# WKV preparation reordered as a pipeline over four channel blocks, with elementwise products on GpSimd

## The reference, cut to what matters

```python
kk = (k * p['k_k']).reshape(B, T, H, N)
kk = kk / jnp.maximum(jnp.linalg.norm(kk, axis=-1, keepdims=True), 1e-12)
for d in range(2):
    w = jnp.exp(-DECAY_SCALE * jax.nn.sigmoid(p['decay_w0'][d] + jnp.tanh(xw @ p['decay_w1'][d]) @ p['decay_w2'][d]))
    a = jax.nn.sigmoid(p['aaa_a0'][d] + (xa @ p['aaa_a1'][d]) @ p['aaa_a2'][d])
    kd = k * (1.0 + (a - 1.0) * p['k_a'])
    y_sum = y_sum + wkv7_scan(rh, w, kdh, vh, -kk, kk * ah, reverse=(d == 1))
    bonus = bonus + jnp.sum(rh * kdh * p['r_k'], axis=-1, keepdims=True) * vh
```

## Time and profile before

| | before |
|---|---|
| median of 3 runs | 2770.46 us |
| lowest, highest | 2763.62, 2773.02 us |
| the profiled execution | 2771.89 us |
| its span | 2770.1 us |
| its mean granted TensorE clock | 0.892 of full speed |
| TensorE matmuls busy | 2271.1 us (82%) |
| VectorE busy | 1157.1 us (42%) |
| ScalarE busy | 763.7 us (28%) |
| GpSimd busy | 334.7 us (12%) |
| stage `prep` | about 562 to 802 us of the span |

### The profile page before, as it was taken

One profiled execution on the slowest core, in us unless ns is written; L12 is line 12 of the kernel. 1 busy time (PEld: TensorE's weight loads), 2 busy tenths in 40 slices (PEclk: granted clock), 3 DMA queues, 4 the chain that ended last, 5 costly groups with the idle time before them and its releaser, 6 DMA issues. The chain is left out here.

```text
span 2770.1 us, 42284 instructions
## 1 busy us (share of the span) xinstructions
PE 2271.1 (82%) x17252; PEld 1898.2 (69%) x17252; DVE 1157.1 (42%) x1619; ACT 763.7 (28%) x1236; POOL 334.7 (12%) x352
## 2 busy tenths in 40 slices
PE   3899997944414768887579986969999999999999
PEld 2788882322203545555568865869999889999987
DVE  4343006646742356767357743422333223332221
ACT  3111110024413214444334422213222212222211
POOL 0000000000000019950544310000000000000000
PEclk9999999966756679999589956989999999999999
DMA  2222210024367210010377424432222333222222
GB/s 85 75 86 86 86 71 35 0 88 193 151 228 222 80 61 1 1 46 11 99 171 186 115 76 148 141 125 76 76 76 80 109 115 111 71 75 76 76 98 89
DMA packets 140716, 262.87 MB, mean 95 GB/s; under 512 B 11024, under 2 KB 89360, under 8 KB 138992
## 3 DMA queue, kind: packets, MB, share of 16 engines
q1 hardware_dynamic: 140592, 261.12, 28.8%
HBM read 189.18 MB, written 68.93 MB: 93 GB/s over the span
## 5 line engine op out<-in xcount | busy, mean ns | idle before, releaser
L203 PE MATMUL ff_acc<-normed_nh,ff_low 128*128 128x320 f32 x1408 | 436.1, 310 | 18.9 <-DVE ff_low L2318 17.7
L204 PE MATMUL ff_acc<-normed_nl,ff_high 128*128 128x320 f32 x1408 | 435.8, 310 | 0.0
L205 PE MATMUL ff_acc<-normed_nh,ff_high 128*128 128x320 f32 x1408 | 435.7, 309 | 0.0
L2318 DVE TENSOR_TENSOR ff_low<-ff_raw,ff_high 128x1024 fp32r<-128x1024 f32 x132 | 161.7, 1225 | 451.6 <-ACT ff_high L2280 451.4
L203 PEld LDWEIGHTS ff_acc<-normed_nh,ff_low 128*128 128x128 f32 x1408 | 264.9, 188 | 19.7 <-issue 19.7
L204 PEld LDWEIGHTS ff_acc<-normed_nl,ff_high 128*128 128x128 f32 x1408 | 265.0, 188 | 0.0
L205 PEld LDWEIGHTS ff_acc<-normed_nh,ff_high 128*128 128x128 f32 x1408 | 264.9, 188 | 0.0
L2280 ACT CAST ff_high<-ff_raw 128x1024 fp32r<-128x1024 f32 x132 | 138.0, 1046 | 255.4 <-PE ff_acc L205 234.0
L204 PE MATMUL ff_acc<-ff_low,ff_hh 128*128 128x512 f32 x440 | 171.2, 389 | 0.0
L203 PE MATMUL ff_acc<-ff_high,ff_hl 128*128 128x512 f32 x440 | 171.2, 389 | 0.0
L205 PE MATMUL ff_acc<-ff_high,ff_hh 128*128 128x512 f32 x440 | 171.2, 389 | 0.0
(11 more groups left out here) (250 smaller groups left out, 4296.8 us busy)
## 6 DMA issues: line engine op xcount, KB each, us to landing
dram_sx<-pr_sx SPq DMA_DIRECT2D x8, 2816.0 KB, 8.1
ff_raw<-in_w_gate SPq DMA_DIRECT2D x44, 512.0 KB, 3.2
ff_raw<-in_w_up SPq DMA_DIRECT2D x44, 512.0 KB, 3.2
ff_raw<-in_w_down SPq DMA_DIRECT2D x44, 512.0 KB, 3.5
si_ab<-dram_sx SPq DMA_DIRECT2D x44, 384.0 KB, 6.9
pj_packed<-in_w_in SPq DMA_DIRECT2D x24, 512.0 KB, 4.3
ch_ops<-dram_sx SPq DMA_DIRECT2D x88, 128.0 KB, 3.5
ch_ops<-dram_sx SPq DMA_DIRECT2D x44, 256.0 KB, 4.5
```

Of the source, the lines that this page charges most:

```text
L203: nc.tensor.matmul(out, ll, rh, start=start, stop=False)
L204: nc.tensor.matmul(out, lh, rl, start=False, stop=False)
L205: return nc.tensor.matmul(out, lh, rh, start=False, stop=stop)
L2318: nc.vector.tensor_tensor(low[s][:, :], raw[s][:, :], high[s][:, :].bitcast(F32), ALU.subtract).then_inc(cut_low[s], 1)
```

## The change

It rewrites the stage `prep`. In it:

- Priming of the semaphores is dropped; counts start at zero.
- VectorE starts each block with the scans and sums of both directions; the bonus of the block before stands behind them; then come the two products `kd` by `k`, then the packed results. The norm `kk` of the next block (`norm_k`) is issued between the results of direction 1, and `floor` and `invert` of the next block ahead of and within direction 0.
- ScalarE takes over the affine step of `kd` (`scale_a`, an Identity activation), puts the square of the next block between the exponentials of the two directions, and runs `root`, `to_rows`, the four sigmoids and the two affine steps of the next block behind the exponentials. The exponential that `r` is multiplied by goes to `sg[d]`, so that `e1` is gone.
- GpSimd takes `av` times `kk` for both directions, `kd[0]` plus `kd[1]`, and the product of that with `r`: four full-width operations a block. The weight `r_k` is folded into four copies of `heads` (`heads_rk`) once at the start.
- SyncE loads `k` and `r` apart from `v`, the first `k` and `r` ahead of the constants; the load for block f+2 is issued behind the stores of block f; the bonus of f is stored in block f+1; each direction's store has a semaphore of its own.

```diff
@@ sync
-                    for d in range(2):
-                        sp.wait_ge(ready, PRIMED + 2 * f + d + 1)
-                        sp.dma_start(g.sx[d, f], ...).then_inc(stored, 16)
-                    sp.wait_ge(bonus, PRIMED + f + 1)
-                    sp.dma_start(g.bonus[f * P:(f + 1) * P, :], kds[:, :]).then_inc(stored, 16)
+                def load_kr(f):
+                    s = f % 2
+                    if f >= 2:
+                        sp.wait_ge(ready, 2 * (f - 1))
+                        sp.wait_ge(kd_summed, f - 1)
...
+                sp.wait_ge(zeroed, 6)
+                load_kr(0)
...
+                load_v(0)
+                load_kr(1)
+                load_v(1)
                 for f in range(FT):
+                    if f >= 1:
+                        store_bonus(f - 1)
+                        if f + 1 < FT:
+                            load_v(f + 1)
+                    for d in both:
+                        sp.wait_ge(ready, 2 * f + d + 1)
+                        sp.dma_start(g.sx[d, f], sx[d][:, :, :, :].rearrange("p c x t -> p (c x t)")).then_inc(sx_stored[d], 16)
+                    if f + 2 < FT:
+                        load_kr(f + 2)
@@ gpsimd
+                for f in range(FT):
+                    s = f % 2
+                    pool.wait_ge(normed, f + 1)
+                    for d in both:
+                        pool.wait_ge(affine, 2 * f + d + 1)
+                        nc.gpsimd.tensor_tensor(av[d][:, :], kk[:, :], av[d][:, :], ALU.mult).then_inc(av_ready, 1)
+                    pool.wait_ge(kd_ready, f + 1)
+                    if f:
+                        pool.wait_ge(bonus_stored, 16 * f)
+                    nc.gpsimd.tensor_tensor(kds[:, :], kd[0][:, :], kd[1][:, :], ALU.add).then_inc(kd_added, 1)
+                    pool.wait_ge(kd_added, f + 1)
+                    pool.wait_ge(kr_in[s], KR * (f // 2 + 1))
+                    nc.gpsimd.tensor_tensor(kds[:, :], r[s][:, :], kds[:, :], ALU.mult).then_inc(kd_summed, 1)
@@ tensor
+                for_w(0, 0)
+                for_a(0, 0)
+                pe.wait_ge(consts, 80)
+                pe.wait_ge(fixed, 1)
+                square_sums(0)
+                for_w(0, 1)
+                for_a(0, 1)
+                spread_norms(0)
                 for f in range(FT):
                     if f + 1 < FT:
                         square_sums(f + 1)
+                        for_w(f + 1, 0)
                         spread_norms(f + 1)
+                        for_a(f + 1, 0)
+                        for_w(f + 1, 1)
+                        for_a(f + 1, 1)
+                    bonus_of(f)
@@ scalar
+                def exponentials(f, d):
+                    act.wait_ge(summed, 2 * f + d + 1)
+                    nc.scalar.activation(tot[:, d, :], tot[:, d, :], ACT.Exp, scale=-DECAY)
+                    nc.scalar.activation(ex[d][:, :], ex[d][:, :], ACT.Exp, scale=-DECAY).then_inc(exped, 1)
+                    nc.scalar.activation(sg[d][:, :], cs[d][:, :], ACT.Exp, scale=-DECAY).then_inc(exped, 1)
+                    act.wait_ge(exped, 4 * f + 2 * d + 2)
+                    nc.scalar.activation(cs[d][:, :], cs[d][:, :], ACT.Exp, scale=DECAY).then_inc(scaled_up, 1)
...
                 for f in range(FT):
+                    more = f + 1 < FT
+                    exponentials(f, 0)
+                    if more:
+                        square(f + 1)
+                    exponentials(f, 1)
+                    if more:
+                        root(f + 1)
+                        to_rows(f + 1)
+                        sigmoid_w(f + 1, 0)
+                        sigmoid_a(f + 1, 0)
+                        sigmoid_w(f + 1, 1)
+                        sigmoid_a(f + 1, 1)
+                        for d in both:
+                            scale_a(f + 1, d)
@@ vector
+                def norm_k(f):
+                    dve.wait_ge(kr_in[f % 2], KR * (f // 2 + 1))
+                    dve.wait_ge(spreads, f + 1)
...
                 for f in range(FT):
+                    sums_of(f, 0)
+                    if f == 0:
+                        floor(0)
+                    sums_of(f, 1)
+                    if f == 0:
+                        invert(0)
+                        norm_k(0)
+                    else:
+                        bonus_of(f - 1)
+                    for d in both:
+                        dve.wait_ge(affine, 2 * f + d + 1)
+                        last = tt(kd[d][:, :], kd[d][:, :], k[s][:, :], ALU.mult)
+                    last.then_inc(kd_ready, 1)
+                    if more:
+                        floor(f + 1)
+                    for d in both:
...
+                        tt(g.etot[:, d, f, :], tot[:, d, :], keep[:, d, :], ALU.mult)
+                        nc.vector.scalar_tensor_tensor(out=o(d, "a"), in0=chunked(kk), scalar=-1.0, in1=chunked(ex[d]),
+                                                       op0=ALU.mult, op1=ALU.mult).then_inc(a_made, 1)
+                        if d == 0 and more:
+                            invert(f + 1)
+                        dve.wait_ge(av_ready, 2 * f + d + 1)
+                        tt(o(d, "b"), chunked(av[d]), chunked(cs[d]), ALU.mult)
+                        if d == 1 and more:
+                            norm_k(f + 1)
+                        dve.wait_ge(kd_ready, f + 1)
+                        tt(o(d, "k"), chunked(kd[d]), chunked(cs[d]), ALU.mult)
+                        tt(o(d, "r"), chunked(r[s]), chunked(sg[d]), ALU.mult).then_inc(ready, 1)
+                bonus_of(FT - 1)
```

More of the change, by code:

```diff
@@ L539, in prep @@
         psa, psb, psq = c.ps("psa", (P, 3 * 512)), c.ps("psb", (P, 3 * 512)), c.ps("psq")
-        consts, zeroed = c.sem("consts"), c.sem("zeroed")
-        loaded = [c.sem(f"loaded{s}") for s in range(2)]
+        consts, zeroed, fixed = c.sem("consts"), c.sem("zeroed"), c.sem("fixed")
+        kr_in, v_in = ([c.sem(f"{n}{s}") for s in range(2)] for n in ("kr_in", "v_in"))
         squared, sums, floored, rooted, inverted, rows, spreads, normed = (
             c.sem(n) for n in ("squared", "sums", "floored", "rooted", "inverted", "rows", "spreads", "normed"))
[L545 to L549, removed]
+        w_prod, a_prod, sig_w, sig_a, affine = (c.sem(n) for n in ("w_prod", "a_prod", "sig_w", "sig_a", "affine"))
+        scanned, mirrored, summed, exped, scaled_up, ready = (
+            c.sem(n) for n in ("scanned", "mirrored", "summed", "exped", "scaled_up", "ready"))
+        kd_ready, av_ready, kd_added, kd_summed, bonus_prod, bonus = (
+            c.sem(n) for n in ("kd_ready", "av_ready", "kd_added", "kd_summed", "bonus_prod", "bonus"))
+        sx_stored = [c.sem(f"sx_stored{d}") for d in range(2)]
+        bonus_stored, a_made = c.sem("bonus_stored"), c.sem("a_made")
         par = lambda name, off: cut(g.par_sb, PCOLS[name] + off, 1)
         chunked = lambda t: t[:, :].rearrange("p (c t) -> p c t", t=CH)
+        both = (0, 1)
+        KR, V = 80, 32
         c.callback(c.reset)
@@ L597, in product, with for_w, for_a @@
                     last.then_inc(sem, 1)
+                def for_w(f, d):
+                    pe.wait_ge(kr_in[f % 2], KR * (f // 2 + 1))
+                    if d or f == 1:
+                        pe.wait_ge(sig_w, 2 * f + d)
+                    elif f >= 2:
+                        pe.wait_ge(bonus, f - 1)
+                    product(psb, w2[f % 2][:, 2 * d, :], g.hid[:, 2 * d, :], w_prod)
+                def for_a(f, d):
+                    if d:
+                        pe.wait_ge(sig_a, 2 * f + 1)
+                    elif f:
+                        pe.wait_ge(normed, f + 1)
+                    product(psa, w2[f % 2][:, 2 * d + 1, :], g.hid[:, 2 * d + 1, :], a_prod)
@@ L607, in spread_norms, with bonus_of @@
+                    pe.wait_ge(sig_a, 2 * max(f, 1))
+                    if f:
+                        pe.wait_ge(normed, f)
                     spread(nc, psa, q, ident, PTOK).then_inc(spreads, 1)
-                pe.wait_ge(consts, PRIMED + 80)
+                def bonus_of(f):
+                    pe.wait_ge(kd_summed, f + 1)
+                    if f + 1 < FT:
+                        pe.wait_ge(sig_w, 2 * f + 4)
+                    else:
+                        pe.wait_ge(bonus, f)
+                    product(psb, heads_rk[:, f, :], kds, bonus_prod)
@@ L616, in _ @@
[L616 to L621, removed]
                     if f + 1 < FT:
                         square_sums(f + 1)
-                    pe.wait_ge(sig_w, PRIMED + 2 * f + 2)
@@ new lines, in sigmoid_a, with scale_a @@
+                def sigmoid_a(f, d):
+                    act.wait_ge(a_prod, 2 * f + d + 1)
+                    if f:
+                        act.wait_ge(ready, 2 * (f - 1) + d + 1)
+                    nc.scalar.activation(av[d][:, :], psa[:, 0:PTOK], ACT.Sigmoid, bias=par("aaa_a0", d * FT + f)
+                                         ).then_inc(sig_a, 1)
```

(25 more changed lines are left out.)

153 lines of the change are left out of this document (66 added, 87 removed).

## The result

| | before | after |
|---|---|---|
| median of 6 runs | 2770.45 us | 2751.24 us |
| lowest, highest | 2763.62, 2773.02 | 2743.68, 2758.86 |
| the profiled execution, its span | 2771.89, 2770.1 | 2743.68, 2741.9 |
| stage `prep`, first fill of padding to first instruction of `solve_in` | 240.0 us | 218.2 us |
| TensorE's granted clock in the stage | 0.64 | 0.55 |

The ratio is 0.993, with a 95% interval of 0.991 to 0.995: 19 us faster where 42 were forecast, and 3 us beyond the slow end of the range. The six runs lie up to 15 us apart, and the profiled execution is the fastest of them, 7.6 us under their median. So I measure on the stage, where the two profiles differ by 21.9 us; another 6.3 us between the two profiled executions lie outside it, where the kernels are the same.

What follows compares the result with a forecast made beforehand. VectorE, the fullest engine, stood idle in a ring of norms, sigmoids, sums, exponentials and results. New blocks of 41.3 us end the stage at 759.8, not 802.2: 2771.9 - 42.4 = 2729.5, less 1.4 gives 2728.1 us; range 2696 to 2748.

Steps and rivals of the forecast that it cites:

- The products' time: TensorE's gate and decay products: 2.36 us apart, the first gate product 2.5; last gate sigmoid ends at T+5.8.
- the ring: Per-block chain from norm through products, sigmoids, exponentials, square and sums to `floor`: 35.4 us without GpSimd's effect on VectorE.
- VectorE's list: VectorE's own work per block: 38.2 us less 8.0 leaves 30.2; about 41.3 with GpSimd's four operations counted in.
- Blocking: In each block, VectorE stands while nearly every GpSimd operation is served: four times 2.8 us.
- the sum of the prediction, 41.4: VectorE's time per block: 30.2 us of work plus four GpSimd operations at 2.8 each.
- GpSimd's operation: One elementwise operation of 1408 columns on GpSimd: 2.9 us, bounds 2.2 and 3.9, giving 2717 and 2745 us.
- The start: Start of the stage: first `k`, `r` land at 570, first scan at 574.2, block 0 ends at 627.1.
- The tail: End of the stage: next stage starts 9.2 us after the last bonus store is issued, at 759.8.
- SyncE's queue: Load of `k`, `r` behind both stores arrives just in time; if 4 us late, two blocks become 2 longer.
- no blocking: Rival: GpSimd's reads fit between VectorE's, blocks take 35.4 us, stage 73.6 less, 2697 us; chance 0.13.
- A smaller gain: Rival: GpSimd operation near 3.9 us, or late loads and bonus stores costing 4 to 10 us; 2740 to 2755; chance 0.12.
- a reordering that doesn't take hold: VectorE still awaits the next norm 5 us or more, `floor` being late through ScalarE; about 2743; no chance of its own.

Runs made afterwards that it cites:

- short products: Changed kernel with the four decay and gate products covering 704 of 1408 columns from block 1 on; blocks 41.7 and 41.6 us, stage 209.9 us.
- experiments two and five: Changed kernel with GpSimd's four operations on 16 columns: stage 192.2 us; changed kernel with those four operations back on VectorE: stage 204.4 us, one run 2730.7 us.
- the run with the last order and a warm TensorE: Changed kernel plus earlier square, decay product first, four operations on VectorE, six added matmuls behind the spread; blocks 38.0 us, stage 191.5 us.

## Why the prediction was wrong

The direction was right and the size was not: the stage was forecast at 197.6 us and took 218.2, 20.6 more. Step by step:

- **The products' time: the step that failed.** The prediction took 2.36 us from the spacing of two sigmoids and carried it to places where TensorE would be doing other things just before. Those rows were made at a clock of 0.94 to 1.00; the clock of 0.65 in the earlier trace rows is a mean of stretches at both levels, which I didn't take apart. At the start of the stage four products lie on the path, each some 2.5 longer: the norm of block 0 ended 46.6 us into the stage, not 36.1. That is 10 of the 20.6 us, read from the rows; no experiment raised the clock there. In a block three products lie on the ring. The last gate sigmoid ended 12.9 us behind the first scan where 5.8 was taken, and `floor` ran 27.5 behind it where 20.4 was taken. That turns 35.4 into some 42.5 and puts the ring above VectorE's list, which I had expected to cover it with 5.9 to spare; one blocking of 2.6 behind `floor`, less 0.6 by which the results there were quicker than the 15 us taken, makes the 44.5. The experiments show this both ways: with short products the block is 41.7, with all three products at the higher clock 41.1.
- **Blocking: right as a mechanism, smaller in blocks 1 and 2.** Forecast 11.2 us a block. In block 0, where VectorE doesn't wait behind its norm, it was 11.6: the two products `kd` took 6.16 instead of 3.15 us, `etot` 3.03 instead of 0.17, and two results 4.37 and 4.57 instead of 1.6. In blocks 1 and 2 it was 5.6, since VectorE now waits 8.6 and GpSimd works in the waits; together 14.2 against 11.2. In the last block it is 4.7 of waits and 8.9 of blocking. That is about 3 us more in each of the three. With short products the sum of the prediction, 41.4, was met (41.7). The rule quoted from the Trainium skill, "SBUF — State Buffer", section "Who interferes with whom", on the shared read interface agrees with the rows after: 6.16 for 3.15, 2.74 for 0.17.
- **GpSimd's operation.** Taken at 2.9, it took 3.15 to 3.18 alone, inside its bounds. The factor of two of the Trainium skill, "GPSIMD Engine Reference", section "Engine selection", an estimate of 3.2, was the better price.
- **The start.** The loads landed 8.6 us into the stage, where 7.8 was taken: 0.8 us.
- **The tail.** 9.8 us from the last store's issue to the next stage, forecast 9.2.
- **SyncE's queue.** `load_kr` behind the stores cost nothing that a wait shows.
- **Two small slips.** 1.0 us more on each GpSimd operation gives 2744 and not 2745, and the DMA engines were 25% busy in the first block only (41 and 42% in the next two). Neither bears on the result.

10.8 up to the first scan of block 1, 3.2 and 3.1 in blocks 1 and 2, 2.8 in the last and 0.6 in the tail make up the 20.6, within rounding.

Of the rivals, "no blocking" was wrong, as experiments two and five show. "A smaller gain" is where the result fell, but not by its causes: no load and no store was late, and GpSimd's operation was near its price. The paragraph on a reordering that doesn't take hold put it at 2743 and named a late `floor`; that came nearest. But it saw the delay in ScalarE's list and the wait at the norm, and VectorE waits for no norm in blocks 1 to 3: the delay came from TensorE's products, and the wait is at `floor` itself. Of the signs that the prediction gave, one of each kind came true: blocked products, which stood for "right", and a wait for `floor` of 3.7 us, which stood near "wrong". They don't exclude each other.

## What to carry to other kernels

Read a duration on TensorE together with the clock of its own window, and ask what will stand ahead of the instruction in the new order; breaking a burst into pieces can double its price. Before moving elementwise work from VectorE to GpSimd, add up the two-input instructions of both as if they were on one engine: the move pays only for what falls into VectorE's waits, and lengthens the rest. When two limits lie within a few us of each other, removing one shows little; only both together show what the ring is worth.

## What was not expected of the hardware

- The same six matmuls of 64 rows took 2.5 us at a clock of 1.00 and 4.9 at 0.50. Three such products, 14.4 us without a gap, ran at 0.50 to their end in the changed kernel, while in the kernel before they ran at 0.94 to 1.00 directly behind a spread of 22 matmuls of 128 rows. In the changed kernel TensorE was idle for 8.6 and 2.8 us between the spread and the products. Six matmuls of 128 rows behind the spread raised the clock to 0.97 to 1.00. With no gap or one of 1.0 us behind them, the products of 64 rows then ran at 1.00 to their end; with 3.3 us of idle time the clock fell to 0.50 during the first of them and stayed there, though TensorE was busy without a gap for the next 9 us. So, as far as these rows go, both count: work of 64 rows held the higher clock but didn't bring it about in 14.4 us, and it was lost behind an idle stretch. Which property of the 64-row products it is was not tried.
- Twelve added matmul instructions a block cost TensorE 5.3 us and made the stage 8 us shorter.
- In the run with the last order and a warm TensorE the clock went from 1.00 to 0.50 during the 64-row product that followed 1.5 us of idle time.
- A VectorE instruction of 22 columns with both inputs in SBUF took 2.74 us in place of 0.17 beside a GpSimd operation of 3.15: width doesn't protect from being blocked.
